# Decode attention by one sequence and four feature tiles, with 2048-byte cache rows

## The reference

```python
h = rmsnorm(x, norm_g)
fq, fk, fv, fz, fl, dq, dk, dv, dz, ga, gb = split(h @ w_in)       # 512 wide each, fl 8, ga and gb 1024
# branch A ("fox"), 8 heads of 64, per-frame causal
s = einsum('bqhd,bkhd->bhqk', q, k_past_and_new) * SCALE + cum_q - cum_k
of = softmax(masked(s)) @ v_past_and_new
# branch B ("diff"), 4 heads of two maps of 64 features, values of 128
s = einsum('bqhmd,bkhmd->bhmqk', q, k_past_and_new) * SCALE + bias[t5_bucket(k - q)]
p = softmax(masked(s)); od = rmsnorm((p[:, :, 0] - lam * p[:, :, 1]) @ v_past_and_new) * (1 - lambda_init)
merged = sigmoid(ga) * ((of * silu(fz)) @ w_up_f) + sigmoid(gb) * ((od * silu(dz)) @ w_up_d)
y = rmsnorm(x + merged @ w_o)
```

## Time and profile before

| | |
|---|---|
| Time, median of 3 runs | 2663.24 us (2660.93 to 2671.53) |
| The profiled execution, its own time | 2669.23 us |
| Its span, first to last instruction | 2667.5 us |
| Mean granted TensorE clock | 0.973 of full speed |
| TensorE busy | 2492.8 us, 93% of the span |
| DVE, ACT, GpSimd busy | 1364.1, 938.5, 392.5 us |
| DMA packets | 586694, of which 330816 under 512 B; 353.03 MB |
| Decode units | from about 590 to 1235 us |

### The profile page before, as it was taken

One profiled execution on the slowest core, in us unless ns is written; L12 is line 12 of the kernel. 1 busy time (PEld: TensorE's weight loads), 2 busy tenths in 40 slices (PEclk: granted clock), 3 DMA queues, 4 the chain that ended last, 5 costly groups with the idle time before them and its releaser, 6 DMA issues.

```text
span 2667.5 us, 35257 instructions
## 1 busy us (share of the span) xinstructions
PE 2492.8 (93%) x13569; PEld 1988.1 (75%) x13569; DVE 1364.1 (51%) x2195; ACT 938.5 (35%) x1837; POOL 392.5 (15%) x398
## 2 busy tenths in 40 slices
PE   7999999996889999979889899899989989999998
PEld 5788888886889999969874565465556556888897
DVE  5311123224343323433247788788778876655543
ACT  4123321121222222100115655664664666422221
POOL 1100001121100000102244103212212340100000
PEclk9999999998999999989989999999999999999999
DMA  5643336558989888987842145055052322544432
GB/s 137 166 123 111 111 109 153 140 143 191 201 213 207 204 189 198 215 182 164 202 132 57 40 92 127 5 128 111 21 123 54 82 68 84 183 142 138 133 123 91
DMA packets 586694, 353.03 MB, mean 132 GB/s; under 512 B 330816, under 2 KB 549896, under 8 KB 580344
## 3 DMA queue, kind: packets, MB, share of 16 engines
q1 hardware_dynamic: 577392, 332.17, 50.8%
q0 software_dynamic: 9136, 18.63, 2.1%
HBM read 250.23 MB, written 100.19 MB: 131 GB/s over the span
## 4 chain that ended last, share of the span: by engine, by line
PE 66%; SPq 13%; DVE 6%; ACT 5%; issue 4%; DMA 4%; POOL 1%; DVEq 0%; ACTq 0%; POOLq 0%
PE p_acc L848 10%; PE p_acc L853 10%; PE p_acc L852 10%; PE a_op L2080 5%; SPq L474 5%; PE a_sb L2055 4%; PE a_sb L2056 3%; PE a_op L2077 3%; PE a_sa L2033 2%; PE a_sa L2036 2%; PE e_U L1397 2%; PE e_U L1398 2%; PE e_U L1399 2%; SPq L348 2%; ACT a_e L1893 2%
## 5 line engine op out<-in xcount | busy, mean ns | idle before, releaser
L848 PE MATMUL p_acc<-p_h_hi,p_w_hi 128*128 128x384 f32 (+1 forms) x1960 | 719.0, 367 | 24.6 <-DVE p_ev L569 19.3
L853 PE MATMUL p_acc<-p_h_hi,p_w_lo 128*128 128x384 f32 (+1 forms) x1920 | 690.5, 360 | 0.0
L852 PE MATMUL p_acc<-p_h_lo,p_w_hi 128*128 128x384 f32 (+1 forms) x1920 | 690.4, 360 | 0.0
L848 PEld LDWEIGHTS p_acc<-p_h_hi,p_w_hi 128*128 128x128 f32 x1960 | 373.3, 190 | 64.5 <-DVE p_ev L569 19.9
L1924 DVE TENSOR_REDUCE a_nmax<-a_sa 128x1 f32<-128x1024 f32 (+7 forms) x384 | 347.1, 910 | 132.2 <-PE a_sa L2038 45.6
L1893 ACT ACTIVATE a_e<-a_sb 128x512 f32<-128x512 f32 (+3 forms) x640 | 310.5, 533 | 285.0 <-PE a_sb L2056 188.2
L853 PEld LDWEIGHTS p_acc<-p_h_hi,p_w_lo 128*128 128x128 f32 x1920 | 364.1, 190 | 30.4
L852 PEld LDWEIGHTS p_acc<-p_h_lo,p_w_hi 128*128 128x128 f32 x1920 | 364.8, 190 | 29.0
L671 DVE TENSOR_TENSOR p_w_lo<-p_raw,p_w_hi 128x1024 fp32r<-128x1024 f32 x96 | 122.1, 1271 | 393.9 <-ACT p_w_hi L602 393.5
L2055 PE MATMUL a_sb<-a_q,a_k 128*128 128x512 f32 (+2 forms) x640 | 277.7, 438 | 20.5 <-ACT a_e L1893 17.9
L602 ACT CAST p_w_hi<-p_raw 128x1024 fp32r<-128x1024 f32 x98 | 102.5, 1046 | 414.2 <-DMA p_raw<-in_w_in 328.3
(11 more groups left out here) (227 smaller groups left out, 3384.6 us busy)
## 6 DMA issues: line engine op xcount, KB each, us to landing
p_raw<-in_w_in SPq DMA_DIRECT2D x98, 512.0 KB, 5.7
s_k_raw<-in_cache_fox_k SPq DMA_DIRECT2D x128, 128.0 KB, 3.9
s_v_raw<-in_cache_fox_v SPq DMA_DIRECT2D x32, 512.0 KB, 7.0
s_k_raw<-in_cache_diff_k SPq DMA_DIRECT2D x128, 128.0 KB, 3.9
s_v_raw<-in_cache_diff_v SPq DMA_DIRECT2D x32, 512.0 KB, 6.9
a_q<-scratch_q_hi SPq DMA_DIRECT2D x32, 512.0 KB, 13.3
a_k<-scratch_k_hi SPq DMA_DIRECT2D x32, 512.0 KB, 15.6
e_pair<-scratch_gT SPq DMA_DIRECT2D x80, 192.0 KB, 2.6
```

Source lines behind the costliest of these rows:

```text
L848: nc.tensor.matmul(acc[a % 2][:, 0:n], hi, h_hi[p][:, k, at:at + n], start=(k == 0), stop=False)
L852: nc.tensor.matmul(acc[a % 2][:, 0:n], hi, h_lo[p][:, k, at:at + n], start=False, stop=False)
L853: last = nc.tensor.matmul(acc[a % 2][:, 0:n], lo, h_hi[p][:, k, at:at + n], start=False, stop=(k == DK - 1))
```

## The change

A unit becomes one sequence and four feature tiles, so that the 512 floats of a key are all used by one unit.

- Keys: 8 transfers, one for each tile t of 128 keys, into 128 partitions, in 2048-byte runs. Partition 32q + r holds key 256q + 32t + r, so the four partition quadrants hold the four quarters of the keys.
- Scores: by products of 32 rows (32 features j of a tile, one quadrant i) by 256 keys, into bank i of a `tab` of four banks, accumulated over the four j. 64 such products replace 16 of 64 rows by 512 keys. The new keys take 16 products instead of 8.
- `q_bd` is loaded in 16 transfers, `kT_new` in 4, `add` in 8 for diff units and 16 for fox units. The values come in one transfer of 2048-byte runs, the new values in one.
- Scores are 4 x 272 = 1088 columns, with the 16 spare columns of three banks set to a large negative number once, instead of 1040.
- `tab` takes four banks, and `turn` has two instead of three.
- The order of events and their slots stay.

```diff
-        k_raw = r_.sb("k_raw", [P, SEQS, 2 * KT, 2, 32])
-        kT = r_.sb("kT", [P, SEQS, 2, PAST // 2])
+        k_raw = r_.sb("k_raw", [P, KT, WIDTH])
+        kT = r_.sb("kT", [P, KT, 4 * FTS, 32])
...
-        tab = s.ps("tab", [P, 3 * 512])
-        turn = [s.ps(f"turn{i}", [P, 512]) for i in range(3)]
+        tab = s.ps("tab", [P, 4, 512])
+        turn = [s.ps(f"turn{i}", [P, 512]) for i in range(2)]
...
-                for b in range(SEQS):
+                keys = cache("k", n).rearrange("(q t r) n -> t q r n", q=4, r=32)
+                for t in range(KT):
                     if n:
-                        sp.wait_ge(k_turned, 2 * (SEQS * (n - 1) + b + 1))
-                    for h in range(2):
-                        for m in range(2):
-                            at = 64 * h + 32 * m
-                            sp.dma_start(k_raw[at:at + 32, b], keys_of(n, b, h, m)).then_inc(k_in[b], 16)
+                        sp.wait_ge(k_turned, KT * (n - 1) + t + 1)
+                    sp.dma_start(k_raw[:, t], keys[t]).then_inc(k_in[t // 2], 16)
...
+                for j in range(4):
+                    rows_j = slice(32 * j, 32 * j + 32)
+                    for i in range(4):
+                        sp.dma_start(q_bd[32 * i:32 * i + 32, j, :, j // 2, :],
+                                     d["qT"][ft:ft + FTS, rows_j, tok].rearrange("f p t -> p f t")).then_inc(small_in, 16)
+                    sp.dma_start(kT_new[P - 32:P, j], d["kT"][ft:ft + FTS, rows_j, tok].rearrange("f p t -> p f t")).then_inc(small_in, 16)
...
+                            sp.dma_start(add[r:r + DEC_SEQ, :, 0:QK], d["nckS"][row:row + 1, 0:PAST].to_broadcast([DEC_SEQ, PAST])
+                                         .rearrange("p (q n) -> p q n", q=4)).then_inc(small_in, 16)
+                            sp.dma_start(add[r:r + DEC_SEQ, 3, QK:QW], d["nckS"][row:row + 1, PAST:KEYS]
+                                         .to_broadcast([DEC_SEQ, DEC_SEQ])).then_inc(small_in, 16)
...
-                for b in range(SEQS):
-                    sp.dma_start(v_raw[:, b], cache("v", n, b).rearrange("(t p) n -> p t n", p=P)).then_inc(v_in, 16)
+                sp.dma_start(v_new[0:DEC_SEQ, :], new[b * DEC_SEQ:(b + 1) * DEC_SEQ, :]).then_inc(v_in, 16)
+                sp.dma_start(v_raw[:], cache("v", n).rearrange("(t p) n -> p t n", p=P)).then_inc(v_in, 16)
...
-            if n >= 3:
-                pe.wait_ge(turn_taken, n - 2)
-            return turn[n % 3]
+            if n >= 2:
+                pe.wait_ge(turn_taken, n - 1)
+            return turn[n % 2]
...
+                for j in range(4):
+                    for i in range(4):
+                        part = slice(32 * i, 32 * i + 32)
+                        for f in range(FTS):
+                            q = q_bd[part, j, f].rearrange("p m t -> p (m t)")
+                            nc.tensor.matmul(tab[f * 32:f * 32 + 32, i, 0:QK], q, kT[part, :, 4 * f + j, :],
+                                             start=(j == 0), stop=(j == 3))
```

More of the change, by code:

```diff
@@ L170, in project @@
     cum_step, nck_stored = s.sem("cum_step"), s.sem("nck_stored")
-    k_in, k_turned = [s.sem(f"k_in{b}") for b in range(SEQS)], s.sem("k_turned")
+    k_in, k_turned = [s.sem(f"k_in{i}") for i in range(4)], s.sem("k_turned")
     small_in, v_in, sel_in, set_made = s.sem("small_in"), s.sem("v_in"), s.sem("sel_in"), s.sem("set_made")
@@ L306, in project, with small_total, cache @@
     last_chunk = lambda g: (g, len(chunks(g)) - 1)
-    OP = 1152
+    scores = tab[:, :, 0:QW]
+    o_sum, o_turned = tab[:, 0, 288:288 + P], tab[:, 1, 288:288 + HD]
     PASS0 = max(acc_at[a] for a in acc_at if a[0] < NT) + 1
-    S_SMALL, S_V, S_K = 16 * 18, 16 * 5, 16 * 4
+    S_V, S_K = 16 * 2, 16 * 2
     def unit(n):
-        return n // 2, n % 2, n // 2 >= 4
-    def cache(name, n, b):
-        ft, g, diff = unit(n)
-        src = d[("cache_diff_" if diff else "cache_fox_") + name][0]
[L320 to L326, removed]
+        return n % DEC_BATCH, n // DEC_BATCH * FTS, n >= DEC_BATCH
+    def small_total(n):
+        return 16 * sum(20 + (8 if unit(i)[2] else 16) for i in range(n + 1))
+    def cache(name, n):
+        b, _, diff = unit(n)
+        src = d[("cache_diff_" if diff else "cache_fox_") + name][0]
+        return src.rearrange("b n h m e -> b n (h m e)" if diff and name == "k" else "b n h e -> b n (h e)")[b]
     def x_rows(t):
@@ L456, in sync @@
                 n = ev_[1]
-                ft, g, diff = unit(n)
+                b, ft, diff = unit(n)
                 if n == 0:
@@ L479, in sync @@
                     sp.wait_ge(maxed, n)
[L480 to L489, removed]
+                tok = slice(SEQ + b * DEC_SEQ, SEQ + (b + 1) * DEC_SEQ)
+                for j in range(4):
[4 more added lines that the diff above has]
+                    sp.dma_start(kT_new[P - 32:P, j], d["kT"][ft:ft + FTS, rows_j, tok].rearrange("f p t -> p f t")).then_inc(small_in, 16)
                 if n == 0:
@@ L769, in vector @@
                 diff = unit(n)[2]
-                dve.wait_ge(small_in, S_SMALL * (n + 1))
+                dve.wait_ge(small_in, small_total(n))
                 if not diff:
-                    tail = add[:, PAST:KEYS]
+                    tail = add[:, 3, QK:QW]
                     nc.vector.tensor_tensor(tail, tail, causal, ALU.add).then_inc(added, 1)
@@ L775, in vector @@
                 dve.wait_ge(scored, n + 1)
[L776 to L777 removed]
+                cut = tab[:, 3, QW - P - DEC_SEQ:QW] if diff else scores
+                term = add[:, 3, QW - P - DEC_SEQ:QW] if diff else add[:]
                 nc.vector.tensor_tensor(cut, cut, term, ALU.add).then_inc(added, 1)
                 dve.wait_ge(added, n + 1 + min(n + 1, 8))
[L780 removed]
+                nc.vector.tensor_reduce(s_stat[:, 0:1], scores, AX.XY, ALU.max, negate=True).then_inc(maxed, 1)
             elif what == "E":
@@ L906, in tensor @@
                 for kt in range(KT + 1):
-                    for b in range(SEQS):
-                        v = v_raw[:, b, kt, :] if kt < KT else v_new[:, b, :]
-                        last = nc.tensor.matmul(tab[b * 32:b * 32 + 32, OP:OP + P], eT[:, kt, b * 32:b * 32 + 32], v,
+                    for f in range(FTS):
+                        v = (v_raw[:, kt] if kt < KT else v_new)[:, f * P:(f + 1) * P]
+                        last = nc.tensor.matmul(o_sum[f * 32:f * 32 + 32], eT[:, kt, f * 32:f * 32 + 32], v,
                                                 start=(kt == 0), stop=(kt == KT))
```

121 lines of the change are left out of this document (59 added, 62 removed).

## The result

The changed kernel takes 2849.25 us (median of 4 runs, 2843.30 to 2858.58) against 2662.09 for the kernel before, a ratio of 1.070 with a 95% interval of 1.066 to 1.074. The prediction was 2695, its range 2634 to 2730. The sign was right and the size was not: +187 us where +31.5 were forecast.

What follows compares the result with a forecast made beforehand. TensorE was taken as the bound, with idle time where SP's burst delays weight loads. Middle 16, first five 5, last three 6, TensorE 2, banks 2.5: +31.5 on 2669.2, 2701; the median, 6.0 lower, 2694.8; range 2634 to 2730.

Steps and rivals of the forecast that it cites:

- Direction and bound: Whole kernel: slower by 31.5 us; TensorE the bound, idle at the decode ends where SP's load burst delays weights.
- Keys on four engines: New key transfers: 4 outermost rows put them on four DMA engines, 22.5 us a unit at 88 ns a row.
- The load of the four engines: Middle units: keys, values, small rows and the rest load each of the four engines 36 to 38.1 us.
- so a unit can't be shorter than this: 37 against 34.96: Eight middle units: weights queue behind keys, so the four engines' load sets the unit, 37 us.
- 8 x 0.48 = 3.9 us where nothing holds it: SP's key loads: eight transfers issued in about 3.9 us, against 12.9 for sixteen before.
- The term for the middle: Eight middle decode units: 37 us each against 34.96, +16 us in all (0 to +25).
- The first five units, +5: Five units ahead of the middle: four engines' load slows them from 41.1 us each, +5 us (0 to +11).
- the last three, +6: Last three decode units: four engines' load slows them from 41.4 us each, +6 us (-5 to +11).
- TensorE, +2: Score step: 128 key-product instructions start 13.6 ns apart, +2 us over 16 units; upper bound 29 ns, +32 us.
- Two banks, +2.5: Start stretch: with two turning banks more transposes wait 0.6 to 1.5 us each, +2.5 us (+1 to +4).
- Small loads: SP's q, kT_new and add loads: 17.2 us in fox units, 13.5 in diff, where 5 us of slack are gained.
- Rival "all 16 engines", 2634: Keys run on all 16 engines, only SP's burst counts, tail idle time goes: about -29 us, 2634; chance 0.21.

Runs made afterwards that it cites:

- with 16 engines: Changed kernel with its keys placed so that each key transfer has 16 outermost rows on the DRAM side instead of 4: 2718.1 us, 1.021 to before.
- the few add loads: Kernel with 16 outermost key rows, plus add loads in 5 transfers per fox unit and only once for diff units: 2678.9 us, 1.006 to before.
- the split: Kernel with 16 outermost key rows and fewer add loads, plus q, kT_new and add loads three chunks later than the keys: 2666.4 us, 1.0013 to before.

## Why the prediction was wrong

- **Direction and bound: right.** SP's burst ahead of the weight load is what slows the ends of before; putting a weight load ahead of the small loads was worth 37 us in the kernel before.
- **Keys on four engines: right**, now shown with 4, 8 and 16 outermost rows at 102, about 205 and 267 to 369 GB/s. The rule of the Trainium skill (DMA: Bandwidth & Descriptors, "Why a DMA increments its semaphore by 16 and not by 1"), the largest number up to 16 that divides both outermost counts, agrees with all three. A row took 77 ns, where 88 were used.
- **The load of the four engines: right in size.** The DMA share of 0.51 over 46.3 us is 377 us of engine time; without 1024 key rows of 77 ns (79), a sixteenth is 18.6, and with 256 key rows (19.7) it is 38.3 a unit, where the prediction had 36 to 38.
- **The step that failed: "so a unit can't be shorter than this: 37 against 34.96", taken as the unit's length, and before it "8 x 0.48 = 3.9 us where nothing holds it".** The prediction let SP issue on while the four engines drain, and so took the larger of the two times. But SP is held with them: beyond four key transfers an issue lasts as long as the drain, 2.46 us, so that no more than that is ever queued ahead, and while the engines run empty (982 to 994 us in the unit shown) SP still has the rest of its 46 issues, of about half a microsecond each, to make. The unit is the sum, 16.8 us held and 25.3 of plain issuing, 42.1, and 4 of waits: 46.3. The sign was there: 12.9 us for 16 key issues was more than the 0.48 of others, and the text passed over it. One by one, the first issues of the first burst of before take 0.33, 0.49, 0.65, 1.75 and 2.31 us, with no wait for a semaphore among them. So SP was held there too, from the fourth transfer on, at 32 rows of 256 bytes for each engine in a transfer. The term for the middle was +16 and measured +88.
- **The first five units, +5, and the last three, +6:** 63 us (13.2 and 50.0) and 27, by the same step.
- **Clock:** not in the sum at all. About 23 us.
- **TensorE, +2: the term was mis-sized.** From the first key product to the next projection product it is 2.94 us (959.83 to 962.77) instead of 1.96, so 15.7 us in all, as measured by the starts. 128 instructions took 2.55 us from start to start (959.83 to 962.38), 19.9 ns each, counted as the prediction counted its 13.6; the 21.6 ns of the expectations have the run of the last one in them. The 13.8 ns of the row at 835.30 belong to products of 16 columns. The upper bound of 29 ns was too high, and the choice of the lower end wrong. The Trainium skill (TensorE: Matmul & The Clock Gate, "Wait — 56ns, not 53.3ns?") has about 25 ns as the least time between starts. That is nearer, but it is undercut here.
- **Two banks, +2.5:** the place was right (+4.0 us at the first key load), the price on the total is 0.
- **Small loads:** 17.2 us forecast in fox units; with 16 engines they take 19.8 (901.2 to 921.1). That diff units gain 5 us from it did not show: with 16 engines the last three took 123.0 instead of 127.2, 1.4 us each.
- **Rival "all 16 engines", 2634:** with 16 engines it was 2718. Of its 84 us of error 13.7 are TensorE's term, 39 went with the few add loads and 13 with the split: SP's burst of 36 or 28 small loads was most of the loss on that side. The rest, 18 us, is open. That large rows free the DMA engines was true (share 0.70 against 0.85 over the stretch), and no run shows a gain from it.

What stays open: why the 4 us that the missing bank costs at the start do not appear in the total, and in what unit the queues are deep. That a full queue is what holds SP is inferred from the lengths of its issues and of the drain; no row shows a queue's filling. It is not a matter of key transfers alone, nor of four engines: with keys by 16 rows the first key issue of the second unit took 8.58 us (at 620.62), behind the values, two stores and two weight loads, and long after its buffer was free (602 us), and in the kernel before the value loads are held 3.0 us a unit.

## What to carry to other kernels

Look at the outermost count of both sides of a transfer before its row size: 2048-byte rows on four engines moved 102 GB/s. Where one engine issues all transfers, its issue time is a resource to be added up: here the issuer was held behind what it had queued, and the time held was added to the rest of its issues, not hidden beside them. A load that the bound engine waits for belongs ahead of a burst or between two halves of it, which is a change of order and here brought 1.4% by itself.

## What was not expected of the hardware

- Once 128 rows of 2048 bytes stood in each of four queues, each further issue on SP took the 2.46 us of its drain; on eight engines, with 128 rows for each in all, the first burst of eight took 5.9 us.
- Products on 32x32 tiles with 256 columns started 19.9 ns apart on average (2.55 us for 128), in the same pattern in either order, and read in runs of 8 or 16 words as fast as in one run (2.76 us in all variants).
- A key transfer on k engines left k + 1 landing records (5 and 9 for k = 4 and 8), and 16 on 16 engines. With fewer than 16 the profile gives no time to landing. So the record count tells on how many engines a transfer ran, where its time is missing.
